# Every half megabyte of the weights as one stretch of memory, in a four-part transformer kernel

## The chip, the cores and the metric

The kernel runs on one core of a Trainium2 chip. The metric is the device time of one execution in microseconds (us). All data is float32 in memory.

## The reference

256 tokens of width 1024 pass through two blocks. The first has two layers: a hybrid mixer (gated linear attention beside compressed, selected and windowed attention), a dense SwiGLU network, a Mamba2 mixer, and a mixture of eight experts, of which each token takes two. The second block has two layers of attention of two kinds side by side. Ahead of each of the six parts a modulation is computed from a condition vector.

```python
def adaln(c, w, b):
    mod = jax.nn.silu(c) @ w + b
    shift, scale, gate = jnp.split(mod[:, None, :], 3, axis=-1)
    return shift, scale, gate
...
def swiglu(h, w_gu, w_down):
    g, u = jnp.split(h @ w_gu, 2, axis=-1)
    return (jax.nn.silu(g) * u) @ w_down
...
    for e in range(N_EXPERTS):
        out = out + gate[..., e:e + 1] * swiglu(h, w_gu[e], w_down[e])
...
    x = second_block(x, c_2, positions_2, pre_norm_gain_2, post_norm_gain_2, w_ada_2, b_ada_2, w_in_2, w_out_2)
```

The weights are some 558 MB, each read once. The expert weights alone are 352 MB.

## The kernel before, in words

Weights are brought by one queue, SP's, in transfers of half a megabyte, 128 partitions of 1024 numbers (4 KB) each. A chunk lands in one of six ring buffers (`ring`). ScalarE rounds it to the format that TensorE multiplies fast (`split_scalar`, L496, tile `sph`), VectorE subtracts the rounded part from the original (`split_vector`, L508, tile `spl`), and TensorE multiplies three times, high by high, low by high and high by low (L519 to L521). There are six buffers each for high and low parts as well. The modulation weights go the same way into the ring, but VectorE multiplies and sums them itself (L569, L572, tile `macc`). They are asked for between the other chunks.

`Stream` lists all chunks of the ordinary weights (`halves`) in the order of their use; `ask` puts chunks of all kinds into the order in which VectorE comes to them. `on_sync` issues them in this order at L478. From the seventh on it first waits until the buffer six chunks back has been used by VectorE:

```python
        if c >= RING:
            sp.wait_ge(*k.when(k.stream.chunks[c - RING][2]))
        sp.dma_start(k.ring[c % RING][:, 0:width], src).then_inc(k.landed[c % RING], 16)
```

In the expert stage each expert takes 14 items of gate and up weights (`moe_gu`, four chunks each) and seven units of down weights (`moe_down`, four chunks each), 84 chunks in all. The down weights of a unit come behind the gate and up weights of later items. Between the splits of chunks the engines do small steps from a list of things in progress: ScalarE applies Silu to an item's result (L2417), VectorE multiplies gate and up (L2423), TensorE turns the result (L529), ScalarE and VectorE split it (L2441, L2450). Tokens for the next expert are gathered in the middle of the present one (L525, L2382, L2387, L2404). Each engine's program is in a fixed order, so a small step stands behind the splits ahead of it.

A second path (`over_sync`, `over_pieces`, L2499 on) handles experts with more than 128 tokens. It is guarded by a value that the router computes, and reads the same expert tensors in pieces of 1 MB.

On the host, `layout` arranges the weights into the arrays that the kernel reads; this is outside the time. Most arrays are slots of 128 rows by 4096 numbers (16 KB a row), and a chunk is a quarter of the columns. A modulation is one array of 128 rows by 24,576 numbers (96 KB), the hybrid projection one of 128 rows by 22,848 numbers. The input x, 256 rows of 1024 numbers, is read in its natural order into two rows of 4 KB for each partition; x and the other small tensors are issued behind the first six chunks, all of which are modulations.

Of the kernel before, what the change touches and what calls it, by code (L numbers as in the profile page):

```python
# [391 lines left out]
class Stream:  # L392
# [3 lines left out]
    def __init__(self, k):  # L396
        d = k.d
        self.halves, self.first, self.chunks, self.chunk_of = [], {}, [], {}
        self.back = []
        for i in range(6):  # L400
            steps, gates = [("step", i, r) for r in range(2 * KD)], [("gate", i, 2 * KD + r) for r in range(KD)]
            late = [] if i == 0 else [("rest", i, r) for r in range(3)] if i == 4 else gates[0:3]
            before = [("gates", i - 1, 0)] if i > 0 else []
            self.back += steps[0:3] + before + steps[3:] + late + [("sum", i, 0)] + [g for g in gates if g not in late]
        self.back += [("rest", 5, 0), ("rest", 5, 1), ("gates", 5, 0)]
        self.at = {}
        at = 0
        for name, n in HYB_ITEMS:
            self.at["hyb", name] = len(self.halves)
            for q in range(2):  # L410
                self.add("hyb", d["hyb_w_in"][:, at + 4 * n * q:at + 4 * n * (q + 1)], 4 * n)
            at += 8 * n
        self.add_slots("hyb_out", d["hyb_w_out"], 0, 2)
        us = units(DENSE_TILES)
        for u in range(-1, len(us)):
            if u + 1 < len(us):
                for j in range(us[u + 1][0] // 2, us[u + 1][0] // 2 + us[u + 1][1] // 2):
                    self.add_slots("dense_gu", d["dense_gu"], j, 1)
            if u >= 0:
                for q in range(us[u][1] // 2):  # L420
                    self.at["dense_down", us[u][0] // 2 + q] = len(self.halves)
                    self.add("dense_down", d["dense_down"][u * 128:(u + 1) * 128, q * HALF:(q + 1) * HALF])
        for j in SSM_ORDER:
            self.add_slots("ssm", d["ssm_w_in"], j, 1)
        self.add_slots("ssm_out", d["ssm_w_out"], 0, 4)
        for q in range(N_EXP * NI + 2):
            if q < N_EXP * NI:
                self.add_slots("moe_gu", d["moe_gu"], q, 1)
            if q % 2 == 1 and q >= 3:
                u = (q - 3) // 2  # L430
                self.at["moe_down", u] = len(self.halves)
                for h in range(2):
                    self.add("moe_down", d["moe_down"][u * 128:(u + 1) * 128, h * HALF:(h + 1) * HALF])
        for l in range(2):
            self.add_slots(f"second{l}", d["w_in2"], 8 * l, 8)
            self.add_slots(f"second_out{l}", d["w_out2"], 2 * l, 2)

    def add(self, name, src, width=HALF):
        self.first.setdefault(name, len(self.halves))
        w = width // 2  # L440
        self.halves += [(src[:, 0:w], w), (src[:, w:width], w)]

    def add_slots(self, name, src, j, n):
        for i in range(j, j + n):
            self.at[name, i] = len(self.halves)
            for q in range(2):
                self.add(name, src[i, :, HALF * q:HALF * (q + 1)])

    def ask(self, key, src, width, freed):

# [99 lines left out]
def back_vector(v, k):  # L550

    if k.at_back["vector"] == len(k.stream.back):
        return
    kind, i, r = k.stream.back[k.at_back["vector"]]
    k.at_back["vector"] += 1
    if kind == "rest":
        return
    S, tick, when = k.S, k.tick, k.when
    mod, bias = k.d["mod"][i], k.V[f"b{i}"]
    if kind in ("step", "gate"):  # L560
        k.stream.ask(("mod", i, r), mod[:, r * QUARTER:(r + 1) * QUARTER], QUARTER, f"mod{i}.step{r}")
        sem, value, w = landed(k, ("mod", i, r))
        n, part, before = (r // 2, r % 2, r - 2) if kind == "step" else (r - 2 * KD, 2, r - 1)
        c = k.st[:, mod_col(i) + n:mod_col(i) + n + 1]
        m = k.macc[:, part * D:(part + 1) * D]
        v.wait_ge(sem, value)
        if n == 0:
            v.wait_ge(*when("c.silu" if i == 0 else f"mod{i - 1}.sum" if kind == "step" else f"mod{i - 1}.gates"))
            v.tensor_scalar(m, w[:, :], c, None, ALU.mult).then_inc(*tick(S.mod_stepped, f"mod{i}.step{r}"))  # L569
        else:  # L570
            v.wait_ge(*when(f"mod{i}.step{before}"))
            v.scalar_tensor_tensor(out=m, in0=w[:, :], scalar=c, in1=m, op0=ALU.mult, op1=ALU.add).then_inc(*tick(S.mod_stepped, f"mod{i}.step{r}"))  # L572
    elif kind == "sum":
        bank = k.banks[k.bank_of.get(f"mod{i}.sum", 0)]
        m = k.mods[:, i, 8:16]
        v.wait_ge(*when(f"mod{i}.sum"))
        v.tensor_tensor(k.mods[:, i, 0:16], bank[:, 0:16], bias[:, 0:16], ALU.add).then_inc(*tick(S.mod_ready, f"mod{i}.summed"))
        v.wait_ge(*when(f"mod{i}.summed"))
        v.scalar_tensor_tensor(out=m, in0=m, scalar=1.0, in1=k.V[f"n{i}"], op0=ALU.add, op1=ALU.mult).then_inc(*tick(S.mod_ready, f"mod{i}.ready"))
    else:  # L580
        bank = k.banks[k.bank_of.get(f"mod{i}.gates", 0)]
        m = k.mods[:, i, 16:24]
        v.wait_ge(*when(f"mod{i}.gates"))
        v.tensor_tensor(m, bank[:, 16:24], bias[:, 16:24], ALU.add).then_inc(*tick(S.mod_ready, f"mod{i}.{'gated' if i < 4 else 'biased'}"))
        if i >= 4:
            v.wait_ge(*when(f"mod{i}.biased"))
            v.tensor_tensor(m, m, k.V[f"post{i - 4}"], ALU.mult).then_inc(*tick(S.mod_ready, f"mod{i}.gated"))
# [715 lines left out]
def compressed_vector(v, k):  # L1303
    S, tick, when, Y = k.S, k.tick, k.when, k.Y
    pe_ = k.V["pe"].rearrange("p (j m) -> p j m", j=2)
    for n in range(10):
        if n < 8:
            k.stream.ask(("cmp", n // 4, n % 4), k.d["cmp_w1"][n // 4, :, QUARTER * (n % 4):QUARTER * (n % 4 + 1)], QUARTER, f"cmp.used{n // 4}.{n % 4}")
        if n == 0 or n == 4:
            j = n // 4  # L1310
            if j == 1:
                v.wait_ge(*when("cmp.used0.3"))
            else:
                v.wait_ge(*when("kv.moved1"))
                v.wait_ge(*when("kv.moved0"))
            for g in range(2):
                for q in range(2):
                    v.tensor_tensor(Y.win[:, 8 * q:8 * q + 8, 15 * g:15 * g + 15], windows(Y.kc2 if j == 0 else Y.vc2, g, q),
                                    pe_[:, j, 8 * q:8 * q + 8].unsqueeze(2).broadcast_to([128, 8, 15]), ALU.add).then_inc(*tick(S.cmp_vector, f"cmp.win{j}"))
        if n < 9:  # L1320
            yield
# [1174 lines left out]
def over_sync(sp, k):  # L2496
# [3 lines left out]
    with sp.If(value > 0):  # L2500
        for e in range(N_EXP):
            for n, (_, src) in enumerate(over_pieces(d, e)):
                c = 42 * e + n
                if c >= 2:
                    sp.wait_ge(S.over_tensor, c - 1)
                sp.dma_start(E.own[c % 2][:, :], src).then_inc((S.over_landed0, S.over_landed1)[c % 2], 16)


def over_pieces(d, e):

    pieces = []
    for u in range(-1, 7):
        if u + 1 < 7:
            pieces += [(("up", 2 * (u + 1) + it, h), d["moe_gu"][14 * e + 2 * (u + 1) + it, :, HALF * h:HALF * (h + 1)])
                       for it in range(2) for h in range(2)]
        if u >= 0:
            pieces += [(("down", u, h), d["moe_down"][(7 * e + u) * 128:(7 * e + u + 1) * 128, HALF * h:HALF * (h + 1)]) for h in range(2)]
    return pieces


# [563 lines left out]
    return t.reshape(n, 4, 128, D).transpose(0, 2, 1, 3).reshape(n * 128, SLOT)  # L3084


def layout(i):
    g = {k: np.asarray(v) for k, v in i.items()}
    a = {}
# [5 lines left out]
             g["pre_norm_gain_2"][1]]  # L3095
    for j in range(6):
        w = mod_w[j].reshape(8, 128, 3, D).transpose(1, 0, 2, 3)
        a[f"mod{j}"] = np.concatenate([w[:, :, 0:2].reshape(128, -1), w[:, :, 2].reshape(128, -1)], 1)
    cols = [fm(g["c"][0]), fm(g["c_2"][0])] + [fm(b) for b in mod_b] + [fm(n) for n in norms]
    cols += [fm(g["post_norm_gain_2"][0]), fm(g["post_norm_gain_2"][1]), fm(g["final_norm"]), fm(g["gla_out_norm"][0])]  # L3100
    cols.append(fm(g["gla_gk_bias"][0]))
# [16 lines left out]
    qb = qb.reshape(D, 2, 4, 64).transpose(0, 2, 1, 3).reshape(D, 512)  # L3118
    kvs = [kv[:, 128 * j:128 * j + 128] for j in range(6)]
    groups = [[kvs[0], kvs[2], kvs[1], kvs[4]], [qb], [kvs[3], kvs[5], lr, gb], [q, k], [v], [r]]  # L3120
    a["hyb_w_in"] = np.concatenate([by_k(np.concatenate(gr, 1)).reshape(128, -1) for gr in groups], 1)
    a["cmp_w1"] = g["nsa_cmp_w1"][0].reshape(2, 16, 128, 256).transpose(0, 2, 1, 3).reshape(2, 128, SLOT)
    a["hyb_w_out"] = down_items(g["hyb_w_out"][0], 8).reshape(2, 128, SLOT)
    a["dense_gu"] = gu_items(g["dense_w_gu"][0], DENSE_TILES)
# [6 lines left out]
    a["moe_down"] = np.concatenate([down_items(g["moe_w_down"][0, e], EXPERT_TILES) for e in range(N_EXP)])  # L3131
    a["w_in2"] = np.concatenate([g["w_in_2"][l].reshape(8, 128, 8, 512).transpose(2, 1, 0, 3).reshape(8, 128, SLOT) for l in range(2)])
    a["w_out2"] = np.concatenate([down_items(g["w_out_2"][l], 8).reshape(2, 128, SLOT) for l in range(2)])
    return {n: np.ascontiguousarray(v) for n, v in a.items()}


# [14 lines left out]
```

## Time and profile before

| | |
|---|---|
| three runs | 2212.88, 2218.41, 2223.59 us |
| median | 2218.41 us |
| profiled execution, its time | 2217.26 us |
| profiled execution, its span | 2215.5 us |
| TensorE busy | 2006.2 us |
| VectorE busy | 1718.0 us |
| ScalarE busy | 1319.8 us |
| moved by DMA | 560.17 MB, mean 253 GB/s |
| granted TensorE clock, mean | 0.951 of full |

The span runs from the first to the last instruction. A wait is the idle time of an engine ahead of an instruction, with what ended it. The chain follows the last instruction back through whatever released each step. Landing is the time from the issue of a transfer to the arrival of its last part.

### The profile page before, as it was taken

What the parts mean: (1) busy time and instruction counts of PE and PEld (TensorE: products, weight loads), DVE (VectorE), ACT (ScalarE), POOL (GpSimd) and SP (SyncE); (2) the same over time, 40 slices, a digit from 0 to 9 for tenths busy, and PEclk for the clock granted to TensorE, in tenths of its full rate; (3) what the DMA queues carried; (4) which work ended last, traced back from release to release, by engine and by line L of the source; (5) the groups of instructions that cost most, each with busy time, mean ns of one, the idle gap of its engine ahead of it and who ended that gap; (6) DMA issues with size and microseconds to landing.
All of it is one profiled execution on the core that took longest, in us unless ns stands there. A gap on an engine that the chain in (4) does not pass through costs nothing.

```text
span 2215.5 us, 28267 instructions
## 1 busy us (share of the span) xinstructions
PE 2006.2 (91%) x10266; PEld 1675.1 (76%) x10266; DVE 1718.0 (78%) x2410; ACT 1319.8 (60%) x1951; POOL 2.0 (0%) x5
## 2 busy tenths in 40 slices
PE   2998899968998799999999999999999986997997
PEld 2786799968887677887778788777778765776775
DVE  5688678658687588988989898898889876786764
ACT  2353434345565387777777787777778764444443
POOL 0000000000000000000000000000000000000000
PEclk9998999978999799999999999999999998998999
DMA  7946489737332289999999899999999982671630
GB/s 271 322 155 198 164 302 318 265 109 257 117 112 89 66 297 324 365 327 345 341 326 358 314 365 330 331 350 325 351 318 357 347 326 84 224 252 59 212 121 19
DMA packets 154066, 560.17 MB, mean 253 GB/s; under 512 B 17217, under 2 KB 17473, under 8 KB 153793
## 3 DMA queue, kind: packets, MB, share of 16 engines
q1 hardware_dynamic: 153920, 558.29, 71.8%
q8 instruction: 84, 1.38, 0.2%
q14 instruction: 62, 0.50, 0.1%
HBM read 557.18 MB, written 1.05 MB: 252 GB/s over the span
## 4 chain that ended last, share of the span: by engine, by line
PE 66%; DVE 14%; DMA 10%; ACT 7%; issue 3%; DVEq 0%; SPq 0%; ACTq 0%
PE ps L519 18%; PE ps L521 18%; PE ps L520 17%; PE ps L525 11%; DVE spl L508 6%; DMA ring<-in_moe_down 6%; ACT sph L496 3%; PE ps L529 2%; DMA ring<-in_moe_gu 2%; DVE macc L572 1%; DMA ring<-in_mod 1%; DMA ring<-in_w_in 0%; DVE arena L1939 0%; DMA ring<-in_hyb_w_in 0%; DVE arena L692 0%
## 5 line engine op out<-in xcount | busy, mean ns | idle before, releaser
L508 DVE TENSOR_TENSOR spl<-ring,sph 128x1024 fp32r<-128x1024 f32 x906 | 1085.3, 1220 | 347.2 <-ACT sph L496 336.3
L496 ACT ACTIVATE sph<-ring 128x1024 fp32r<-128x1024 f32 x906 | 952.6, 1059 | 632.9 <-PE ps L521 432.3
L519 PE MATMUL ps<-sph,hH 128*128 128x512 f32 (+1 forms) x1296 | 527.3, 407 | 4.9 <-DVE hL L2404 3.1
L521 PE MATMUL ps<-sph,hL 128*128 128x512 f32 (+1 forms) x1296 | 508.6, 392 | 0.0
L520 PE MATMUL ps<-spl,hH 128*128 128x512 f32 (+1 forms) x1296 | 507.1, 391 | 0.0
L519 PEld LDWEIGHTS ps<-sph,hH 128*128 128x128 f32 x1296 | 246.5, 190 | 57.5 <-issue 10.4
L519 PE MATMUL ps<-sph,rH 128*128 128x512 f32 x664 | 277.3, 418 | 13.9 <-DVE rL L2931 4.4
L521 PEld LDWEIGHTS ps<-sph,hL 128*128 128x128 f32 x1296 | 245.5, 189 | 52.9
L520 PEld LDWEIGHTS ps<-spl,hH 128*128 128x128 f32 x1296 | 246.5, 190 | 50.6 <-issue 3.8
L520 PE MATMUL ps<-spl,rH 128*128 128x512 f32 x664 | 266.4, 401 | 0.0
L521 PE MATMUL ps<-sph,rL 128*128 128x512 f32 x664 | 266.4, 401 | 0.0
L529 PE MATMUL ps<-cst,arena 128*128 128x128 f32 (+2 forms) x640 | 124.5, 309 | 95.7 <-DVE arena L684 48.1
L525 PE MATMUL ps<-arena 128*128 128x128 f32 (+6 forms) x1004 | 182.3, 326 | 15.5 <-DVE arena L2098 6.1
L519 PE MATMUL ps<-hH,sph 128*128 128x256 f32 x640 | 187.5, 293 | 7.4 <-DVE spl L508 5.0
L529 PEld LDWEIGHTS ps<-cst,arena 128*128 128x128 f32 (+2 forms) x640 | 87.5, 157 | 137.7 <-DVE arena L684 52.1
L520 PE MATMUL ps<-hL,sph 128*128 128x256 f32 x640 | 184.8, 289 | 0.0
L521 PE MATMUL ps<-hH,spl 128*128 128x256 f32 x640 | 184.6, 288 | 0.0
L525 PEld LDWEIGHTS ps<-arena 128*128 128x128 f32 (+2 forms) x1004 | 135.3, 198 | 49.5 <-issue 36.3
L572 DVE SCALAR_TENSOR_TENSOR macc<-ring,st,macc 128x1024 f32<-128x1024 f32 x126 | 161.1, 1280 | 14.2 <-DMA ring<-in_mod 13.9
L519 PEld LDWEIGHTS ps<-sph,rH 128*128 128x128 f32 x664 | 129.8, 195 | 43.3 <-DVE rL L2931 4.8
L521 PEld LDWEIGHTS ps<-sph,rL 128*128 128x128 f32 x664 | 129.3, 195 | 28.7
L520 PEld LDWEIGHTS ps<-spl,rH 128*128 128x128 f32 x664 | 130.3, 196 | 26.5 <-issue 1.2
(289 smaller groups left out, 1649.2 us busy)
## 6 DMA issues: line engine op xcount, KB each, us to landing
ring<-in_moe_gu SPq DMA_DIRECT2D x448, 512.0 KB, 6.0
ring<-in_moe_down SPq DMA_DIRECT2D x224, 512.0 KB, 6.1
ring<-in_mod SPq DMA_DIRECT2D x144, 512.0 KB, 5.4
ring<-in_w_in SPq DMA_DIRECT2D x64, 512.0 KB, 4.9
ring<-in_dense_gu SPq DMA_DIRECT2D x44, 512.0 KB, 5.9
ring<-in_ssm_w_in SPq DMA_DIRECT2D x40, 512.0 KB, 4.6
ring<-in_dense_down SPq DMA_DIRECT2D x22, 512.0 KB, 5.8
ring<-in_hyb_w_in SPq DMA_DIRECT2D x20, 512.0 KB, 6.3
```

Of the source, the lines that this page charges most:

```text
L496: a.activation(k.high[m % SPLITS][:, 0:w], raw[:, 0:w], ACT.Copy).then_inc(k.S.half_rounded, 1)
L508: v.tensor_tensor(k.low[m % SPLITS][:, 0:w], raw[:, 0:w], k.high[m % SPLITS][:, 0:w], ALU.subtract).then_inc(*k.tick(k.S.half_split, f"hal ...
L519: pe.matmul(out, a[0], b[0], start=start, stop=False, skip_group_check=True)
L520: pe.matmul(out, a[0], b[1], start=False, stop=False, skip_group_check=True)
L521: return pe.matmul(out, a[1], b[0], start=False, stop=stop, skip_group_check=True)
L525: return pe.matmul(out, a, b, start=start, stop=stop, skip_group_check=True)
L529: return pe.transpose(out, in_, k.C["ident"][0:n, 0:n])
L572: v.scalar_tensor_tensor(out=m, in0=w[:, :], scalar=c, in1=m, op0=ALU.mult, op1=ALU.add).then_inc(*tick(S.mod_stepped, f"mod{i}.step{r}"))
```

## The change

Each chunk becomes one contiguous piece of memory. On the host the arrays get a new axis for the quarter (or, for a modulation, the 24th part) ahead of the partition axis, and the kernel picks a piece with an index where it cut columns. The order of the chunks, their sizes and their destinations stay. `add` now takes one chunk where it took two. The hybrid projection becomes a flat array with its pieces one behind the other.

```diff
-            for q in range(2):
-                self.add("hyb", d["hyb_w_in"][:, at + 4 * n * q:at + 4 * n * (q + 1)], 4 * n)
-            at += 8 * n
+            for q in range(4):
+                self.add("hyb", d["hyb_w_in"][at:at + 256 * n].rearrange("(p n) -> p n", p=128), 2 * n)
+                at += 256 * n
...
-                    self.add("dense_down", d["dense_down"][u * 128:(u + 1) * 128, q * HALF:(q + 1) * HALF])
+                    for h in range(2):
+                        self.add("dense_down", d["dense_down"][u, 2 * q + h])
...
-                for h in range(2):
-                    self.add("moe_down", d["moe_down"][u * 128:(u + 1) * 128, h * HALF:(h + 1) * HALF])
+                for h in range(4):
+                    self.add("moe_down", d["moe_down"][u, h])
...
-    def add(self, name, src, width=HALF):
+    def add(self, name, src, width=QUARTER):
+
         self.first.setdefault(name, len(self.halves))
-        w = width // 2
-        self.halves += [(src[:, 0:w], w), (src[:, w:width], w)]
+        self.halves.append((src, width))
...
-            for q in range(2):
-                self.add(name, src[i, :, HALF * q:HALF * (q + 1)])
+            for q in range(4):
+                self.add(name, src[i, q])
...
-        k.stream.ask(("mod", i, r), mod[:, r * QUARTER:(r + 1) * QUARTER], QUARTER, f"mod{i}.step{r}")
+        k.stream.ask(("mod", i, r), mod[r], QUARTER, f"mod{i}.step{r}")
...
-            k.stream.ask(("cmp", n // 4, n % 4), k.d["cmp_w1"][n // 4, :, QUARTER * (n % 4):QUARTER * (n % 4 + 1)], QUARTER, f"cmp.used{n // 4}.{n % 4}")
+            k.stream.ask(("cmp", n // 4, n % 4), k.d["cmp_w1"][n // 4, n % 4], QUARTER, f"cmp.used{n // 4}.{n % 4}")
...
-                sp.dma_start(E.own[c % 2][:, :], src).then_inc((S.over_landed0, S.over_landed1)[c % 2], 16)
+                sp.dma_start(E.own[c % 2].rearrange("p (q n) -> p q n", q=2), src.rearrange("q p n -> p q n")).then_inc((S.over_landed0, S.over_landed1)[c % 2], 16)
...
+def in_pieces(w, n):
+
+    j, p, width = w.shape
+    return w.reshape(j, p, n, width // n).transpose(0, 2, 1, 3)
...
-        a[f"mod{j}"] = np.concatenate([w[:, :, 0:2].reshape(128, -1), w[:, :, 2].reshape(128, -1)], 1)
+        a[f"mod{j}"] = in_pieces(np.concatenate([w[:, :, 0:2].reshape(128, -1), w[:, :, 2].reshape(128, -1)], 1)[None], 24)[0]
...
-    a["hyb_w_in"] = np.concatenate([by_k(np.concatenate(gr, 1)).reshape(128, -1) for gr in groups], 1)
+    a["hyb_w_in"] = np.concatenate([in_pieces(by_k(np.concatenate(gr, 1)).reshape(1, 128, -1), 4).ravel() for gr in groups])
...
+    for n in ("cmp_w1", "hyb_w_out", "dense_gu", "dense_down", "ssm_w_in", "ssm_w_out", "moe_gu", "moe_down", "w_in2", "w_out2"):
+        a[n] = in_pieces(a[n].reshape(-1, 128, SLOT), 4)
```

## Rows read from the trace of the kernel before

**Rows 1.** The page: DMA queue and its share, chain by engine.

```profile
q1 hardware_dynamic: 153920, 558.29, 71.8%
...
PE 66%; DVE 14%; DMA 10%; ACT 7%; issue 3%; DVEq 0%; SPq 0%; ACTq 0%
```

**Rows 2.** Waits of the whole span: total us, times, longest us.

```profile
ACT sph L496 <- PE ps L521: 432.3, 301, 12.2
```

**Rows 3.** Waits from 850 to 1800 us, the expert stage.

```profile
DVE spl L508 <- ACT sph L496: 113.4, 142, 3.2
ACT sph L496 <- DMA ring<-in_moe_gu: 84.8, 175, 1.9
...
ACT sph L496 <- DMA ring<-in_moe_down: 62.3, 103, 2.6
...
PE ps L529 <- DVE arena L2423: 22.7, 13, 3.4
```

**Rows 4.** The chain from 860 to 882 us: start, us, what.

```profile
869.22 6.64 DMA ring<-in_moe_down
...
875.88 1.06 ACT sph L496
...
878.20 0.34 DVE arena L2423
...
878.67 0.41 PE ps L529 x2
...
879.42 0.23 PE ps L520
...
880.50 0.43 PE ps L521
```

**Rows 5.** Timeline of VectorE at the first and last of seven stalls.

```profile
867.98 7.12 DVE L508 TENSOR_TENSOR spl<-ring,sph 128x1024 fp32r<-128x1024 f32 x6
876.97 1.23 DVE L508 TENSOR_TENSOR spl<-ring,sph 128x1024 fp32r<-128x1024 f32 x1 [1.88 <-ACT sph L496]
...
1659.00 1.23 DVE L508 TENSOR_TENSOR spl<-ring,sph 128x1024 fp32r<-128x1024 f32 x1 [2.40 <-ACT sph L496]
```

**Rows 6.** Windows: length, each engine's busy us, then PEclk, DMA share, GB/s.

```profile
879.00:884.00 5.00, 5.00 (x16) 3.98 (x16) 5.00 (x6) 3.53 (x6) 0.00 (x0) 0.66 0.96 346
...
1531.00:1536.00 5.00, 5.00 (x23) 4.13 (x22) 5.00 (x7) 4.23 (x6) 0.00 (x0) 1.00 0.90 308
...
800.00:806.00 6.00, 5.26 (x24) 4.01 (x24) 5.16 (x6) 5.59 (x8) 0.00 (x0) 1.00 0.96 375
```

**Rows 7.** Waits from 780 to 850 us, the first expert.

```profile
PE ps L529 <- DVE arena L2423: 1.9, 3, 0.7
```

**Rows 8.** Windows of other stretches, read for DMA share and GB/s.

```profile
0.00:9.00 9.00, 0.00 (x0) 0.00 (x0) 2.49 (x6) 1.50 (x2) 0.20 (x4) 1.00 0.79 259
...
4.00:9.00 5.00, 0.00 (x0) 0.00 (x0) 2.12 (x5) 0.00 (x0) 0.00 (x0) 1.00 1.00 338
...
9.00:13.00 4.00, 0.00 (x0) 0.00 (x0) 4.00 (x4) 0.00 (x0) 0.00 (x0) 1.00 1.02 417
...
20.00:38.00 18.00, 3.58 (x17) 3.62 (x18) 12.79 (x10) 4.29 (x11) 0.00 (x0) 1.00 1.03 409
...
880.00:979.00 99.00, 99.00 (x432) 80.04 (x431) 88.97 (x98) 75.01 (x90) 0.00 (x0) 0.98 0.97 348
```

**Rows 9.** DMA issues at 203 to 209, 625 to 700, 850 to 1800 us; last: landing.

```profile
ring<-in_mod SPq DMA_DIRECT2D x2, 512.0 KB, 3.5
...
ring<-in_ssm_w_out SPq DMA_DIRECT2D x14, 512.0 KB, 4.0
...
ring<-in_moe_gu SPq DMA_DIRECT2D x407, 512.0 KB, 6.0
```

**Rows 10.** The chain of the whole span, two long pieces near the start.

```profile
8.11 14.61 DMA ring<-in_mod
...
81.68 8.28 DMA ring<-in_hyb_w_in
```

More of the change, by code:

```diff
@@ L2513, in over_pieces @@
         if u + 1 < 7:
-            pieces += [(("up", 2 * (u + 1) + it, h), d["moe_gu"][14 * e + 2 * (u + 1) + it, :, HALF * h:HALF * (h + 1)])
+            pieces += [(("up", 2 * (u + 1) + it, h), d["moe_gu"][14 * e + 2 * (u + 1) + it, 2 * h:2 * h + 2])
                        for it in range(2) for h in range(2)]
         if u >= 0:
-            pieces += [(("down", u, h), d["moe_down"][(7 * e + u) * 128:(7 * e + u + 1) * 128, HALF * h:HALF * (h + 1)]) for h in range(2)]
+            pieces += [(("down", u, h), d["moe_down"][7 * e + u, 2 * h:2 * h + 2]) for h in range(2)]
     return pieces
```

## Prediction

> **What bounds the kernel now.** I read the page first, then the waits of the whole run, then stretches of it. TensorE is busy for 2006 of 2215.5 us, and the one queue that streams the weights keeps the 16 DMA engines busy for 71.8% of the span [rows 1]. The chain that ended last is 66% TensorE and 10% DMA, so the change can touch a tenth of the path directly. Next come the two splitting engines. ScalarE rounds each half megabyte (L496) and VectorE subtracts (L508); ScalarE's longest wait, 432 us, is for TensorE [rows 2], which costs nothing.
>
> The stage to study is the mixture of experts, eight experts of 84 transfers each, from 783 to 1806 us. TensorE consumes a transfer with six matmuls of 128x512 that start 0.23 us apart, 1.37 us in all [rows 4]. The rows of the chain show those steps. Expert follows expert every 130.1 us (the seven long stalls below stand at 878.67 and at 1660.71, with five in between, six steps of 130.3), or 1.55 us per transfer. In the 950 us from 850 to 1800, ScalarE waits 147 us for transfers (84.8 + 62.3), yet TensorE waits for one thing alone, VectorE's L2423, for 22.7 us [rows 3]. So nearly all the lateness of DMA is absorbed, and the rest comes out at one place per expert.
>
> The chain around 875 us says how [rows 4]. A transfer of moe_down asked for at 869.22 lands 6.64 us later. ScalarE had been idle for it and rounds it at once, VectorE splits it at 876.97 [rows 5], and only behind that split, because its program is in order, comes L2423, for which TensorE had stopped. TensorE restarts at 878.67, and shortly after, its matmuls stand 0.43 instead of 0.23 us apart. The granted clock of that stretch is 0.66: the lower of the two levels for part of it [rows 6]. This happens seven times, and the seven long stalls add up to 19.9 us. The remaining 2.8 us of the 22.7, and 1.9 us in the first expert [rows 7], are short stalls of the same kind.
>
> **The change part by part.** It moves no work. Transfers, bytes, order, destinations, semaphores and the 4 KB that each partition receives stay, so SP's issue time and all instructions cost the same. It adds no wait. What changes is where the 128 pieces of 4 KB lie: one beside the other, where they were 16 KB apart (modulations 96 KB, the hybrid projection 89 KB). The rearranging is done on the host, before the measured time. The path for overfull experts (L2499 and on) issued no transfer in this trace, so its new form costs nothing here. Three things in the trace tell what the distance does.
>
> First, transfers that travel alone [rows 9]. With nothing else in flight, modulations at a distance of 96 KB land after a median of 3.5 us, and ssm_w_out at 16 KB after 4.0. Same bytes, same destinations in form, both beside busy compute engines. So the source's layout matters, by 0.5 us.
>
> Second, rates of a full queue [rows 8]. From 20 to 38 us, modulations and hyb_w_in: 409 GB/s. From 880 to 979 us, expert weights at 16 KB: 348 GB/s at a share of 0.97, which is 359 at full share. One half megabyte (524,288 bytes) takes 1.28 us of the one and 1.46 us of the other.
>
> Third, the layout that the change gives to all weights exists already in one tensor. X is 2 x 128 rows of 4 KB, each 128 in one stretch, and is the transfer behind the first six modulations. Those six and the parameters are 3.35 MB, and 2.33 MB (259 GB/s for 9 us) have passed by 9 us; so of the next 4 us the first 2.4 are the end of the modulations and the rest is X, and together they run at 417 GB/s, above the 409 that modulations reach by themselves: 1.26 us per half megabyte [rows 8]. No slow part for X is hidden in that. It is the nearest row to the new layout, so I take it: 1.26 instead of 1.46 us per transfer in the experts, and for a lone transfer 3.5 us or a little less instead of 4.0. The caution is that TensorE and ScalarE were idle then.
>
> With a service time of 1.26 us DMA is faster than the 1.37 us in which TensorE wants the next one, where it now is slower. The queue behind a transfer then hardly builds, and the landing time in the experts (median 6.0 us, [rows 9]) should fall to 4 to 5 us.
>
> What that is worth:
>
> *The seven long stalls.* In the first, VectorE sat idle 1.9 us before the late split, in the last 2.4 [rows 5]; over the seven it is 13.6 us. With the data there in time, L2423 moves up by just this, and no further, since VectorE's own run of six splits (7.12 us, 1.19 each) stands before it [rows 5]. For the full sum the transfer asked for at 869.22 must be landed and rounded by 875.1, so land within 4.8 us. Bounds: 0 and 13.6. I take 11, four fifths, since some transfers will still be late in a burst.
>
> *The half-speed stretch.* The window with granted clock 0.66 loses 5 x 0.34 = 1.7 us [rows 6]. Six of the seven long stalls have one behind them, one has not (1531 to 1536, clock 1.00). Shortened by 1.9 us, the stalls are 0.7 to 1.3 us; the stall of 0.7 us that lies between 800 and 806 us left the clock at 1.00 [rows 6]. Bounds: 0 and 10.2. The stalls to come are nearer to the 0.7 than to the 2.6 to 3.4 us of the present ones, so I take 10.
>
> *Short stalls.* 4.7 us in all (2.8 + 1.9), bounds 0 and 4.7; I take 2, since half of them have no idle VectorE before them.
>
> *Start and hybrid stage.* Before the first matmul the path waits for modulations, 14.61 us in one piece [rows 10]. The stretch 4 to 9 us ran at 338 GB/s; at 417 it would be 1 us shorter. In the hybrid stage the path holds one transfer of 8.28 us (81.68), of which I give back 2, as in the long stalls. Bounds 0 and 6; I take 3.
>
> *All the rest.* Dense, state-space and second block: their weights arrive early or behind TensorE's own work. Nothing, covered by TensorE; it would cost at most the 0.5 us per lone transfer if that cover were gone.
>
> Sum: 11 + 10 + 2 + 3 = 26 us. The profiled execution took 2217.3 us (span 2215.5 and 1.8 around it), 1.1 us under the median of 2218.41. 2217 - 26 = 2191 us. With every term at its upper bound, 34 us, it is 2183; a saving that grew beyond VectorE's idle time is excluded by its order of work.
>
> The Trainium skill ("DMA: Bandwidth & Descriptors", Latency and other measured facts) has a row that bears on this. It finds copies of 128-row tiles slower only at large power-of-two distances, from 2 MiB on by a fifth or more, and at nearly full rate at 512 KiB; the remedy it names is a padded row distance or tiles laid out contiguously. By that list, distances of 16 and 96 KB should cost nothing, and the sum would be zero. The trace differs, with 3.5 against 4.0 us for lone transfers [rows 9], and I go by the trace.
>
> **The rivals.**
>
> *The layout isn't the cause.* The expert stage may run at 359 GB/s because ScalarE, VectorE and TensorE use the memory on chip that the packets are written to, and because the ring of six lets only four or so be in flight. For it: from 4 to 9 us modulations ran at 338 GB/s, and the same tensor at 409 later, so something else than distance slows transfers as well [rows 8]. Against it: lone transfers are slower at 16 KB in the midst of equal work. If 0.5 us per transfer is won but the queue's rate stays, the long stalls shorten by 0.5 us each, 3.5 us, and no clock is kept: 2213 us; if nothing is won, 2217. The skill's row above gives this outcome too, as a rule on distance.
>
> *One stretch is slower.* The pieces asked for together would lie in 512 KB, where they lay in 2 MB, and modulations in 12 MB. The rows could also be read as "the narrower, the slower": 12 MB at 409, 2 MB at 359. If the step repeated, the rate would be 359 x 359 / 409 = 315 GB/s, 1.66 us per transfer. Its place is the expert stage, and it decides from 1.55 us (338 GB/s), the pace that the stage has now, only 6% below today's rate. Beyond that DMA is the bound, and 672 transfers x 0.11 us give 74 us: 2291 us. At half that step (1.56 us) it is 7 us and longer stalls, some 2230. Against it stands X, at 417 GB/s from one stretch.
>
> *The stalls shorten but the clock still drops.* 16 us without the 10: 2201 us. This is inside my forecast's case, as its weak end.
>
> **How the numbers follow.** The forecast's case (2183 to 2205 us, likeliest 2191) has 0.58: two independent rows, lone transfers and X, point the same way. The layout not being the cause, 2208 to 2220 us, has 0.31. One stretch being slower has 0.11, with times from 2225 to 2291. A measurement of this kernel can tell about 0.5%, 11 us, from no change; below 2207 is faster. The forecast's case counts as faster nearly whole, 0.57; the slower case gives 0.10; the rest, 0.33, is same. The range: leaving out the slower case (0.11) and a tenth at the other ends, 2182 to 2221 us.
>
> **What would show each step right or wrong.** Right: lone transfers of ssm_w_out land after 3.5 us or less; expert transfers have a median of 4 to 5 us; ScalarE's waits for moe_gu and moe_down fall from 147 us to under 60; the waits for L2423 fall from 22.7 to 8 to 12 us; the granted clock in the experts stays at 1.00 behind them; expert follows expert in 127 us. Rival one: these landing times stay within 0.3 us of the old ones. Rival two: landing above 6.5 us, DMA share 1.00 and an expert in more than 131 us. The prediction would be wrong in its middle step if landing times fall as said and the L2423 waits don't, which would mean that VectorE was late by its own work.

## The result and the profile after

| | before | changed |
|---|---|---|
| median of four runs | 2219.02 us | 2185.22 us |
| lowest and highest | 2212.88, 2223.59 us | 2184.13, 2193.01 us |
| profiled execution | 2217.26 us | 2193.01 us |

The ratio is 0.9857, with a 95% interval of 0.9824 to 0.9890: 34 us faster in the median, which the interval makes 24 to 39 us, and 24 us in the profiled executions. 2191 was forecast. The profiled execution of the changed kernel is the slowest of its four; its mean granted clock was 0.950, and 0.956 to 0.959 in the others.

The page of the changed kernel: the queue and the chain by engine. Lines in the code have moved by one.

```profile
q1 hardware_dynamic: 153920, 558.29, 70.9%
...
PE 76%; DVE 12%; ACT 5%; DMA 3%; issue 3%; DVEq 0%; SPq 0%; ACTq 0%
```

Packets and bytes are the same as in [rows 1]. DMA's share of the chain fell from 10% to 3%, TensorE's rose from 66% to 76%. Waits of the changed kernel from 850 to 1800 us, to be held against [rows 3]:

```profile
ACT sph L497 <- DMA ring<-in_moe_gu: 34.7, 98, 1.5
ACT sph L497 <- DMA ring<-in_moe_down: 34.5, 74, 2.6
...
PE ps L530 <- DVE arena L2424: 9.1, 8, 2.5
```

ScalarE waits 69 us for expert transfers where it waited 147, and TensorE's wait for the multiplication on VectorE fell from 22.7 to 9.1 us. In the first expert, before 850 us, this wait is gone altogether, where [rows 7] had 1.9. Its first long stall, in the chain from 864 to 880 us (start, us, what):

```profile
867.85 4.74 DMA ring<-in_moe_down
...
874.94 0.34 DVE arena L2424
...
875.41 0.41 PE ps L530 x2
...
877.10 0.23 PE ps L522
```

and VectorE's timeline there:

```profile
866.60 6.90 DVE L509 TENSOR_TENSOR spl<-ring,sph 128x1024 fp32r<-128x1024 f32 x6
873.71 1.23 DVE L509 TENSOR_TENSOR spl<-ring,sph 128x1024 fp32r<-128x1024 f32 x1 [0.21 <-ACT sph L497]
```

It is the same place as in [rows 4, 5]. The late transfer took 4.74 us where it took 6.64, VectorE stood idle for 0.21 us where it had 1.88, and the step of 0.43 us between matmuls did not come. TensorE in the timeline at the first and the longest stall (the number in brackets is its idle time), and windows behind them (columns as in [rows 6]):

```profile
875.41 0.41 PE L530 MATMUL ps<-cst,arena 128*128 128x128 f32 x2 [1.05 <-DVE arena L2424]
...
1383.91 0.41 PE L530 MATMUL ps<-cst,arena 128*128 128x128 f32 x2 [2.53 <-DVE arena L2424]
```

```profile
879.00:884.00 5.00, 5.00 (x24) 4.13 (x23) 5.00 (x7) 4.57 (x6) 0.00 (x0) 1.00 1.02 410
1383.00:1388.00 5.00, 4.09 (x19) 3.40 (x20) 4.88 (x7) 4.13 (x6) 0.00 (x0) 1.00 0.98 359
```

The first stall is 1.05 us instead of 2.93. All seven are still there: 1.05, 1.7, 0.8, 0.8, 2.53, 0.8 and 1.1 us, 8.8 where they were 19.9. Behind the longest one the clock stayed at 1.00 too. From the first to the last of them an expert takes 126.9 us, where it took 130.3. Next, transfers (from 625 to 700, and 850 to 1800 us) and the window to be held against the last of [rows 8]:

```profile
ring<-in_ssm_w_out SPq DMA_DIRECT2D x14, 512.0 KB, 3.3
...
ring<-in_moe_gu SPq DMA_DIRECT2D x405, 512.0 KB, 5.3
```

```profile
880.00:979.00 99.00, 99.00 (x457) 80.79 (x456) 89.60 (x99) 75.42 (x88) 0.00 (x0) 1.00 0.97 363
```

Against [rows 9], a lone transfer of ssm_w_out is 0.7 us faster and an expert transfer 0.7 us. The two modulations of [rows 9] are not: 3.6 us now, 3.5 before. Last, the whole expert stage, before and changed (length; TensorE's busy us and matmuls come first, then the columns of [rows 6]):

```profile
779.25:1811.20 1031.95, 1003.67 (x4526) 815.25 (x4527) 899.44 (x971) 788.03 (x979) 0.00 (x0) 0.99 0.94 340
...
780.61:1783.99 1003.38, 991.66 (x4527) 808.19 (x4527) 893.15 (x971) 788.44 (x979) 0.00 (x0) 1.00 0.94 349
```

The stage from the first expert matmul to the first of the last unit ran from 779.25 to 1811.20 us before and from 780.61 to 1783.99 now: 1032.0 and 1003.4 us, 28.6 us less. TensorE's idle time in it fell by 16.5 us (28.3 to 11.7), its busy time for the same matmuls by 12.0. The whole saving of the stage is more than the difference of the two profiled executions (24.3); the stages ahead of it and behind it were 1.4 and 2.9 us longer. Those stages vary by as much on their own: together they took between 1180 and 1188 us in the five profiled executions of this document that have this layout outside the experts and six or eight buffers, and 1184 to 1187 in three with the old one.

### The profile page after: what moved, and what is told of

The parts are those of the page before. It is cut to its first block, busy times and chain, and to the rows that moved or that the text cites. A ratio compares the mean times of both kernels' runs of the same rounds, so it can differ in the third digit from the quotient of the medians.

```text
span 2191.2 us, 28267 instructions
## 1 busy us (share of the span) xinstructions
PE 2000.5 (91%) x10266; PEld 1673.1 (76%) x10266; DVE 1712.2 (78%) x2410; ACT 1320.3 (60%) x1951; POOL 2.0 (0%) x5
## 3 DMA queue, kind: packets, MB, share of 16 engines
HBM read 557.18 MB, written 1.05 MB: 255 GB/s over the span
## 4 chain that ended last, share of the span: by engine, by line
PE 76%; DVE 12%; ACT 5%; DMA 3%; issue 3%; DVEq 0%; SPq 0%; ACTq 0%
PE ps L520 21%; PE ps L522 21%; PE ps L521 21%; PE ps L526 11%; DVE spl L509 4%; PE ps L530 3%; ACT sph L497 2%; DVE macc L573 2%; DMA ring<-in_moe_down 1%; DMA ring<-in_mod 1%; DVE arena L1940 0%; DVE arena L693 0%; ACT ps L703 0%; DVE arena L685 0%; DVE arena L799 0%
## 5 line engine op out<-in xcount | busy, mean ns | idle before, releaser
L573 DVE SCALAR_TENSOR_TENSOR macc<-ring,st,macc 128x1024 f32<-128x1024 f32 x126 | 161.0, 1279 | 11.4 <-DMA ring<-in_mod 11.1
```

## The experiments

**Which weights.** The first run gives stretches to the two expert tensors alone, the second to all others alone. The kernel's loops are those of the changed kernel; a tensor with the old layout gets the new indices by a view (the hybrid projection its old columns). Shown is the first run's edit, shortened.

```diff
-    for n in ("cmp_w1", "hyb_w_out", "dense_gu", "dense_down", "ssm_w_in", "ssm_w_out", "moe_gu", "moe_down", "w_in2", "w_out2"):
+    for n in ("moe_gu", "moe_down"):
         a[n] = in_pieces(a[n].reshape(-1, 128, SLOT), 4)
...
+    for n in ("cmp_w1", "hyb_w_out", "dense_gu", "dense_down", "ssm_w_in", "ssm_w_out", "w_in2", "w_out2"):
+        d[n] = d[n].rearrange("j p (q n) -> j q p n", q=4)
```

> Only the two expert tensors (moe_gu, moe_down) lie in stretches; all other weights lie as before. Theory (the gain is made in the expert stage, through earlier landings): the whole gain is there, a ratio of 0.983 to 0.989 to the kernel before, median landing of the expert transfers 5.3 us, waits for L2423 (or its line here) 8 to 12 us, no lower clock behind them. Rival (the gain is spread over all stages, or came with the modulations' layout): a ratio of 0.993 or above.

> All weights but the experts' lie in stretches; the expert tensors keep their distance of 16 KB. Theory: 0.998 to 1.001, since lone transfers land 0.7 us sooner in the other stages but behind other work; the seven long stalls stay at some 20 us. Rival (spread gain): 0.993 or below.

Experts alone: 2193.56 us, ratio 0.9877 (0.9854 to 0.9901), L2424 waits 8.3 us from 850 to 1780. The others alone: 2215.38 us, ratio 0.9988 (0.9974 to 1.0002), L2424 waits 22.4 us, landings of 6.1 us. The expert stage, from the same matmul to the same as above, took 1005.8 us in the first run and 1031.1 in the second, against 1032.0 before and 1003.4 in the changed kernel. So nearly all that was measured is in the expert tensors, 25 us of it against 3 in the rest, and whether the rest brings anything is below what was measured.

**How many buffers.** The kernel before and the changed one with five ring buffers, and with eight; with eight, the pairs of buffers for the split parts were cut from six to five, so that the memory stays the same. The five-buffer edit changes the first constant alone, to 5; for eight, two semaphores were added as well.

```diff
-RING = 6
+RING = 8
...
-SPLITS = 6
+SPLITS = 5
```

> The kernel before with five ring buffers instead of six. Theory (in the expert stage the loop of buffer freed, asked for, landed, rounded, split must close within the stage's pace): with a landing time of 5.2 to 6 us and 2.3 us of rounding and splitting, five buffers give one transfer per 1.5 to 1.66 us against the pace of 1.55; the kernel gets 30 to 90 us slower, and L2423 waits rise well over 23 us. Rival (stalls come from VectorE's own order, not from landings): less than 8 us slower.

> The changed kernel with five ring buffers. Theory: a landing time that is 0.7 us shorter closes the loop in 1.36 to 1.52 us; it loses 5 to 50 us to the changed kernel, and less than the kernel before loses by the same edit, so that the distance between the two layouts grows from 34 us to 45 or more. Rival (landing times don't decide): the distance stays at 34.

> The changed kernel with eight ring buffers and five pairs of buffers for the split parts, the same memory on chip. Theory (the stalls that remain come from the loop of ring buffers, of which six are too few for a burst): the waits for L2424 fall below 5 us and 10 to 20 us are saved, a ratio to the kernel before of 0.976 to 0.981. Rival (the remaining stalls are VectorE's own work, and one pair fewer of split buffers costs): no faster than the changed kernel, 0.985 or above.

> The kernel before, at its distances of 16 and 96 KB, with eight ring buffers and five pairs for the split parts. Theory: with eight buffers the landing time of 6 us no longer matters, most of the seven stalls and the lower clock behind them go, and the old layout is within 5 us of the new one at eight buffers. Rival (the layout acts apart from the ring): the distance between the layouts stays at 25 to 34 us.

| buffers | layout before | stretches | difference |
|---|---|---|---|
| 5 | 2353.47 us, 1.0603 (1.0573 to 1.0632) | 2252.84 us, 1.0160 (1.0126 to 1.0194) | 101 us |
| 6 | 2219.02 us | 2185.22 us, 0.9857 (0.9824 to 0.9890) | 34 us |
| 8, and 5 pairs | 2188.68 us, 0.9879 (0.9858 to 0.9901) | 2185.55 us, 0.9871 (0.9850 to 0.9893) | 3 us |

Each ratio is to the kernel before, timed beside the run: a median of 2218.72 us for five buffers and 2215.02 for eight. Five buffers cost more than expected, 135 us in the old layout and 68 in the new. Their landings stayed at 6.0 and 5.3 us, and from 850 to 1780 us TensorE waited 85.7 us for L2423 in the old layout and 38.0 us for L2424 in the new. With eight buffers, the old layout is as fast as the new one within the intervals. Its transfers are no quicker; they are asked for earlier. Issues and waits of the old layout with eight buffers, 850 to 1780 us:

```profile
ring<-in_moe_gu SPq DMA_DIRECT2D x405, 512.0 KB, 6.6
```

```profile
ACT sph L496 <- DMA ring<-in_moe_gu: 10.9, 27, 1.8
PEld ps L519 <- DVE spl L508: 8.2, 14, 0.9
...
ACT sph L496 <- DMA ring<-in_moe_down: 4.3, 10, 1.6
```

A landing of 6.6 us, yet only 15 us of waits for it. The second line is new: with five pairs of split buffers TensorE's weight loads wait 14 times for VectorE, 8.1 us in the new layout as well. The matmuls' waits for L2423 or L2424 are gone in both. The expert stage with eight buffers, in the new layout and in the old:

```profile
776.33:1777.01 1000.68, 995.94 (x4527) 808.34 (x4527) 890.34 (x971) 787.24 (x979) 0.00 (x0) 1.00 0.94 350
...
779.62:1780.31 1000.69, 995.88 (x4526) 808.87 (x4526) 891.07 (x971) 787.49 (x979) 0.00 (x0) 1.00 0.94 350
```

It is equally long in both, and only 2.7 us shorter than in the changed kernel with six buffers, though 9.1 us of waits for L2424 are gone. TensorE idled 7.0 us less there, and was busy 4.3 us longer with the same matmuls. Of these 4.3, 1.7 us are a lower clock in the first 8 us of the stage (0.79); the rest may be the weight loads that wait, which is not shown. So the 10 to 20 us expected of eight buffers on top of the new layout did not come, and at most a part of that can be the cut of the pairs. Eight buffers with six pairs were not run.

**What distance does.** The first run of this part is a kernel that only loads expert weights and leaves the whole computation out. So do the three further loading kernels below; the second of the four also runs TensorE, VectorE and ScalarE without pause on unrelated buffers. Each was executed once. `step` is the distance in KB, and `m` pieces of 4 KB share a row:

```python
def piece(flat, step, i):
    m = step // 4
    width = 256 * step
    at = (i // m) * 128 * width
    row = flat[at:at + 128 * width].rearrange("(p n) -> p n", p=128)
    q = i % m
    return row[:, 1024 * q:1024 * (q + 1)]
```

> A kernel that only loads: for distances between the 128 rows of 4, 8, 16, 20, 32, 96, 128 and 512 KB in turn, 36 transfers of half a megabyte with six in flight, then 8 that travel alone; all other engines are idle. Theory (distance decides): about 415 GB/s and 3.3 us alone at 4 KB, less and 4.0 us alone at 16 KB. If powers of two are what matters, 20 and 96 KB are as good as 4 KB, and 32, 128 and 512 KB as bad as 16 or worse. If width does, time falls from 16 KB on to 512 KB. Rival (the layout isn't the cause): all distances within 2%.

> The same loads while TensorE, VectorE and ScalarE work without pause on other buffers. Theory: the order of the distances is that of the idle run, rates nearly the same. Rival (busy engines slow the landing): every distance, 4 KB too, falls from about 410 to some 360 GB/s.

Windows of the idle kernel while six transfers are in flight, for 4, 16, 20, 96 and 512 KB (length, VectorE, GpSimd, PEclk, DMA share, GB/s):

```profile
12.00:50.00 38.00, 0.00 (x0) 0.00 (x0) 1.00 1.03 411
165.00:203.00 38.00, 0.00 (x0) 0.00 (x0) 1.00 1.02 408
246.00:285.00 39.00, 0.00 (x0) 0.00 (x0) 1.00 1.03 410
402.00:440.00 38.00, 0.00 (x0) 0.00 (x0) 1.00 1.03 410
553.00:590.00 37.00, 0.00 (x0) 0.00 (x0) 1.00 1.03 411
```

The rates don't differ. Alone, the eight transfers took 3.2 us at 4 KB, 3.5 at 8, 3.9 at 16, 3.6 at 20, 3.4 at 32 and 96, 3.2 at 128 and 3.4 at 512 KB. With the engines busy, 4, 16 and 20 KB gave 410, 407 and 410 GB/s in like windows, and alone 3.2, 3.9 and 3.5 us. Neither theory was right as it stood: with six in flight distance costs nothing, alone 16 KB costs 0.7 us, and busy engines cost next to nothing. The expert stage has neither one nor six in flight. Hence the next kernel.

> A kernel that only loads, 24 transfers at each of 1, 2, 3, 4 and 5 in flight, for distances of 4, 16, 20 and 112 KB in turn. The full queue moved 410 GB/s at every distance, but alone a transfer took 3.2 us at 4 KB and 3.9 at 16 KB. Theory (distance costs through parts of one transfer that end late, which a full queue covers): at 1 to 3 in flight 16 KB is slower than 4 KB by 10 to 20%, at 4 by a few per cent, at 5 by nothing; 20 and 112 KB lie between, nearer to 4 KB. Rival (only alone does the distance matter): no difference from 2 in flight on.

Its windows from the first issue at one depth to the first at the next, empty ends included: at 4 KB with 1, 4 and 5 in flight, then the same at 16 KB:

```profile
5.50:82.90 77.40, 0.00 (x0) 0.00 (x0) 1.00 0.48 163
...
175.20:209.80 34.60, 0.00 (x0) 0.00 (x0) 1.00 0.93 364
209.80:244.40 34.60, 0.00 (x0) 0.00 (x0) 1.00 0.93 364
244.40:340.10 95.70, 0.00 (x0) 0.00 (x0) 1.00 0.40 131
...
443.70:481.40 37.70, 0.00 (x0) 0.00 (x0) 1.00 0.90 334
481.40:515.90 34.50, 0.00 (x0) 0.00 (x0) 1.00 0.93 365
```

The rate at 16 KB is lower by 20, 12, 9 and 8% with one to four in flight, and the same with five. At four, landings are 5.2 us at 4 KB and 5.7 at 16; 20 and 112 KB are as good as 4 there (372 and 373 GB/s). That the loss shrinks with the number in flight and is gone at five is as expected.

**Is it the stretch, or only not 16 KB?** The rest as in the changed kernel, but the expert rows padded to 20 KB, or laid out in rows of 28 pieces, 112 KB (the edit for 20 KB is shown):

```diff
-        a[n] = in_pieces(a[n].reshape(-1, 128, SLOT), 4)
+        t = a[n].reshape(-1, 128, SLOT)
+        a[n] = np.zeros((len(t), 128, SLOT + QUARTER), np.float32)
+        a[n][:, :, 0:SLOT] = t
...
+        d[n] = d[n][:, :, 0:SLOT].rearrange("j p (q n) -> j q p n", q=4)
```

> The expert rows get 4 KB of padding, so that the pieces of 4 KB lie 20 KB apart; all other weights lie in stretches as in the changed kernel. If the power of two is what costs, this is as fast as the changed kernel (ratio 0.983 to 0.989). If only neighbouring pieces help, it is as slow as experts at 16 KB (0.998 to 1.001).

> The expert pieces lie 112 KB apart (28 pieces to a row, as the modulations had 24); the rest as in the changed kernel. The modulations landed alone in 3.5 us before, against 4.0 at 16 KB and 3.3 in stretches. Theory (a landing time of 3.5 is most of the way): ratio 0.985 to 0.993. Rival (only a stretch helps): 0.998 to 1.001.

20 KB: 2188.15 us, ratio 0.9893 (0.9867 to 0.9918). 112 KB: 2190.54 us, ratio 0.9895 (0.9871 to 0.9919). Landings were 5.4 and 5.5 us, L2424 waits 8.1 and 7.3. The expert stage took 1004.0 and 1003.9 us, against 1003.4 in stretches and 1032.0 at 16 KB. So padding alone does all but 0.6 us of what the stage gained. One more loading kernel looked around 16 KB:

> The loading kernel once more, 24 transfers at 1 and at 4 in flight, for distances of 12, 15, 16, 17, 24, 48, 64 and 80 KB. 4, 20, 32, 96, 112, 128 and 512 KB gave 3.2 to 3.6 us alone, and those tried at 4 in flight gave 403 to 407 GB/s; 16 KB gave 3.9 to 4.0 us and 360 GB/s. Theory (16 KB alone is bad, by its exact value): 15 and 17 KB are already at 3.6 us or less and at 395 GB/s or more, as are all the others. Rival (a range around 16 KB, or the small multiples of 16 KB, are bad): 15 and 17, or 48 and 80 KB, give 3.8 us or more and 380 GB/s or less.

Windows for 15, 16 and 17 KB, alone and at four in flight:

```profile
122.40:206.10 83.70, 0.00 (x0) 0.00 (x0) 1.00 0.49 150
206.10:240.20 34.10, 0.00 (x0) 0.00 (x0) 1.00 0.94 369
240.20:334.80 94.60, 0.00 (x0) 0.00 (x0) 1.00 0.40 133
334.80:372.30 37.50, 0.00 (x0) 0.00 (x0) 1.00 0.90 336
372.30:456.90 84.60, 0.00 (x0) 0.00 (x0) 1.00 0.48 149
456.90:490.20 33.30, 0.00 (x0) 0.00 (x0) 1.00 0.96 378
```

Only 16 KB stands out: 3.9 us alone and 336 GB/s at four in flight, against 3.5 us and 369 to 378 GB/s a kilobyte to either side. 12, 48, 64 and 80 KB gave 3.4 to 3.6 us and 368 to 374 GB/s; only 24 KB was somewhat lower at four in flight, 353. The rates named in the expectation are from windows without the empty ends; in such windows the seven other distances gave 395 to 411 GB/s and 16 KB 370, so the expectation held. (4 KB, which it puts at 403 or more, had 391 in such a window.)

## Why the prediction was right, and where not

**The place.** It named seven stalls of the expert stage, and the chain through them. Both runs with a part of the tensors agree: with the experts in stretches the stalls shrink, without they stay. That landing time against the number of buffers is the cause is shown from both sides, since one buffer fewer trebles the difference between the layouts and two more remove it.

**The long stalls.** 11 us were taken, of a bound of 13.6 in VectorE's idle time; 11.1 were saved. The stall at 875 us shortened by 1.88 us, where the text expected it to shorten by VectorE's idle time and no further. That idle time fell by 1.67 us, and the run of six splits before it was itself 0.22 us shorter (6.90 against 7.12), so the equality with the old idle time of 1.88 is chance. The fifth stayed at 2.53 us: its transfer, issued at 1374.86, still took 6.23 us.

**The lower clock.** 10 us were taken. In windows of 4 us over the whole expert stage, one minus the clock times the length adds up to 10.3 us before, all of it behind six stalls, and to nothing now. The argument, that short stalls don't lower the clock, was weaker than it looked: behind the stall of 2.53 us it stayed too, as it had behind one of the seven before.

**The short stalls** gave 4.4 us (4.7 to 0.3), where 2 were taken. The reason for taking half was wrong: those with no idle VectorE directly ahead of them, such as the one of 0.7 us between 818 and 823 us, went too.

**Start and hybrid stage** were to give 3 us. The piece of 8.28 us in [rows 10] fell to 7.07, but the 14.61 us at the start became 14.57, and the expert stage began 1.4 us later than before. So at the places named a little over 1 us came, nearly all in the hybrid stage, and the time of the kernel doesn't tell whether it reached the end: the run with all but the experts in stretches gained 3 us with an interval of 0 to 6. The 1 us at the start rested on 338 GB/s from 4 to 9 us; the changed kernel has 344 there, so the slow first transfers have another cause.

The four terms came to 26 us. The expert stage alone gave 28.6 us: 16.5 of idle time (11.1 in the long stalls, 4.4 in the short, 1.0 in the last wait of the stage, 3.57 to 2.58 us) and 12.0 of busy time. Of the latter 10.3 are the clock; the remaining 1.7 us were not followed. That 2191 lies so near to the times is partly luck. Twice as much from the short stalls, and 2.7 us that no term held, made up for the start. And the 34 us of the medians are as much as all upper bounds together, though the long stalls kept 8.8 us and the start gave next to nothing. What the medians show beyond the 28.6 us of the expert stage is within their interval, and no trace here places it.

**The step that failed** is the price of a transfer. The text read 409 GB/s for modulations, 359 for experts and 417 for X as rates that distance sets, and took 1.26 us instead of 1.46 per half megabyte. The same reading of the changed kernel, 363 GB/s at a share of 0.97, gives 374 GB/s or 1.40 us, which is still above TensorE's 1.37. With six in flight every distance moves 408 to 411 GB/s. What differed in those rows was the number in flight. An estimate from landing time over pace makes it five from 20 to 38 us (6.3 over 1.28 us) and four in the expert stage (6.0 over 1.55). Distance does act at four, by 8%, and the landing time in the stage fell by 0.7 us to 5.3, not to between 4 and 5. ScalarE's waits for transfers fell to 69 us, where under 60 was said. The sum survived because the stalls needed less than that: the first deciding transfer had to land within 4.8 us and took 4.74, half a microsecond less than the median.

**The rivals.** That a stretch is slower is refuted by 410 GB/s and the shortest time alone. That the layout isn't the cause is refuted by the runs with a part of the tensors. Half of the caution behind it was right, that something besides distance sets the rate: the number in flight. The rule of the Trainium skill ("DMA: Bandwidth & Descriptors", Latency and other measured facts) gives slower rates only for large powers of two. At 512 KB, where that row has nearly full rate, the loading kernel agrees (411 GB/s with six in flight); its silence on small distances was no evidence that 16 KB is free. Its remedy, padding by 4 KB, worked here at 16 KB too: 0.9893 of the time.

## What to carry to other kernels

Before the layout of a streamed tensor is changed, look at how long a transfer takes to land against how many can be asked for ahead: here 0.7 us per transfer was worth 101, 34 or 3 us with five, six or eight buffers. A rate is to be compared only with one at the same number in flight. A late transfer costs where an engine's fixed order puts a small step, for which another engine waits, behind the work on it, and that step can be found by following the one wait of the bounding engine.

## What was not expected of the hardware

One distance is bad, and its neighbours are not. 128 pieces of 4 KB that lie 16 KB apart took 3.9 to 4.0 us alone, at 15 and 17 KB 3.5, and in one stretch 3.2; at four in flight the rates were 336, 369 and 378, and 364 GB/s. 64 and 128 KB, powers of two as well, were among the best (3.4 and 3.2 us). Why 16 KB is slow stays open; no run here tells. And engines that were busy without pause on other buffers took at most 1 GB/s from a full queue: 410, 407 and 410 at 4, 16 and 20 KB, where the idle kernel had 411, 408 and 410.
